# The last expert's second product in eight column tiles, with the FFN's first tiles loaded between them, and VectorE's order at two places

## The reference

```python
def expert_choice_moe(h, w_router, w_gate, w_up, w_down):
    ...
    a = jnp.einsum('becd,edf->becf', xg, w_gate)
    u = jnp.einsum('becd,edf->becf', xg, w_up)
    y = jnp.einsum('becf,efd->becd', jax.nn.silu(a) * u, w_down)
    y = y * top_w[..., None].astype(y.dtype)
    return ...scatter-add of y over the tokens...

x = x + g2 * expert_choice_moe(h2, ...)      # end of block one
return rms_norm(x, final_g)                  # into block two

f = swiglu(rmsnorm(h, g[0]), ffn_gate[i, 0], ffn_up[i, 0], ffn_down[i, 0])
h = h + MACARON * rmsnorm(f, g[1])
```

## Time and profile before

| | |
|---|---|
| time, median of 3 runs | 2323.99 us (2323.2 to 2325.95) |
| the profiled execution's own time | 2323.81 us |
| its span | 2322.5 us |
| TensorE busy | 2010.2 us (87%) |
| VectorE busy | 983.5 us (42%) |
| ScalarE busy | 669.7 us (29%) |
| DMA | 647.48 MB, mean 279 GB/s |
| chain that ended last, by engine | PE 51%, DMA 20%, SP's queue 17%, DVE 7% |

### The profile page before, as it was taken

One profiled execution on the slowest core, in us unless ns is written; L12 is line 12 of the kernel. 1 busy time (PEld: TensorE's weight loads), 2 busy tenths in 40 slices (PEclk: granted clock), 3 DMA queues, 4 the chain that ended last, 5 costly groups with the idle time before them and its releaser, 6 DMA issues.

```text
span 2322.5 us, 29242 instructions
## 1 busy us (share of the span) xinstructions
PE 2010.2 (87%) x12336; PEld 1339.5 (58%) x12336; DVE 983.5 (42%) x1219; ACT 669.7 (29%) x812; POOL 66.7 (3%) x144
## 2 busy tenths in 40 slices
PE   7999999666666666666678999999999999999998
PEld 4767972111111111111136999779998999788997
DVE  3744661000000000000004656876658656876656
ACT  3433430000000000000003444564435444465444
POOL 0000000000000000000001000000001000100000
PEclk8999999777777777777789999999999999999999
DMA  7345899999999999999998565335554554425552
GB/s 305 120 176 202 338 377 421 421 421 421 420 421 420 421 421 420 420 421 420 421 421 331 188 204 173 132 118 182 192 193 160 182 194 170 170 78 186 192 190 90
DMA packets 91363, 647.48 MB, mean 279 GB/s; under 512 B 10144, under 2 KB 10656, under 8 KB 14304
## 3 DMA queue, kind: packets, MB, share of 16 engines
q1 hardware_dynamic: 91232, 645.61, 71.2%
HBM read 644.52 MB, written 1.05 MB: 278 GB/s over the span
## 4 chain that ended last, share of the span: by engine, by line
PE 51%; DMA 20%; SPq 17%; DVE 7%; ACT 2%; issue 2%; POOL 1%; DVEq 0%; ACTq 0%; POOLq 0%
SPq L2821 16%; PE PS L449 13%; PE PS L451 13%; PE PS L450 13%; DMA XR<-in_mu 4%; DMA front<-in_mu 3%; PE PS L907 3%; DMA QT<-in_mu 2%; DMA XT<-in_mu 2%; DMA ring<-in_mu 2%; DMA ring<-in_fg 1%; DMA XT<-in_md 1%; DMA c_dft<-in_mu 1%; DVE low L1846 1%; DMA ring<-in_wq 1%
## 5 line engine op out<-in xcount | busy, mean ns | idle before, releaser
L1846 DVE TENSOR_TENSOR low<-ring,WH 128x2048 fp32r<-128x2048 f32 (+1 forms) x163 | 372.1, 2283 | 181.6 <-ACT WH L2235 179.1
L449 PE MATMUL PS<-XH,WH 128*128 128x256 f32 x1408 | 396.9, 282 | 3.6 <-DVE XL L1878 3.6
L450 PE MATMUL PS<-XL,WH 128*128 128x256 f32 x1408 | 395.1, 281 | 0.0
L451 PE MATMUL PS<-XH,low 128*128 128x256 f32 x1408 | 393.1, 279 | 0.0
L2235 ACT ACTIVATE WH<-ring 128x2048 fp32r<-128x2048 f32 (+1 forms) x164 | 313.1, 1909 | 29.2 <-DMA ring<-in_fg 22.9
L449 PEld LDWEIGHTS PS<-XH,WH 128*128 128x128 f32 x1408 | 264.5, 188 | 7.2 <-issue 5.4
L451 PEld LDWEIGHTS PS<-XH,low 128*128 128x128 f32 x1408 | 267.4, 190 | 0.0
L450 PEld LDWEIGHTS PS<-XL,WH 128*128 128x128 f32 x1408 | 264.6, 188 | 1.4
L1828 DVE TENSOR_TENSOR T1S<-T1S,PS 128x512 f32<-128x512 f32 x16 | 11.0, 688 | 536.6 <-PE PS L907 536.6
L2501 ACT ACTIVATE T1S<-PS 128x512 f32<-128x512 f32 x16 | 9.6, 597 | 547.7 <-PE PS L907 547.7
L449 PE MATMUL PS<-WH,FH 128*128 128x512 f32 x352 | 139.6, 396 | 0.4 <-DVE FL L1976 0.4
(11 more groups left out here) (453 smaller groups left out, 3132.9 us busy)
## 6 DMA issues: line engine op xcount, KB each, us to landing
ring<-in_fg SPq DMA_DIRECT2D x44, 1024.0 KB, 4.9
ring<-in_fu SPq DMA_DIRECT2D x44, 1024.0 KB, 4.9
ring<-in_fd SPq DMA_DIRECT2D x44, 1024.0 KB, 4.8
ring<-in_mu SPq DMA_DIRECT2D x39, 1024.0 KB, 26.9
ring<-in_md SPq DMA_DIRECT2D x39, 1024.0 KB, 27.1
ring<-in_mg SPq DMA_DIRECT2D x36, 1024.0 KB, 27.2
ring<-in_wmod SPq DMA_DIRECT2D x24, 1024.0 KB, 6.1
ahead<-in_mg SPq DMA_DIRECT2D x14, 1024.0 KB, 27.4
```

Source lines behind the costliest of these rows:

```text
L449: t.matmul(o, l[0], r[0], start=start, stop=False, skip_group_check=True)
L450: t.matmul(o, l[0], r[1], start=False, stop=False, skip_group_check=True)
L451: return t.matmul(o, l[1], r[0], start=False, stop=stop, skip_group_check=True)
L1846: own(v.tensor_tensor(low[:, w.slot.index, 0:size], w.flat, WH[:, w.slot.index, 0:size].bitcast(f32), ALU.subtract).then_inc(*c.wl.up()), ...
```

## The change

The second product of expert 15 is taken by output columns. Its 8 MB are laid out as eight tiles, each with all of the contraction for 128 output columns, and each column q goes through everything at once: product (16 matmuls into bank 2), T1, scatter into 128 columns of banks 4 to 7, copy to XR, two transposes into bank 3, then ScalarE scales by the final gain into XH and VectorE makes XL in one operation from the same bank. fg0 and fu0 are queued between md124, md125 and md126, their splits are made by ScalarE and VectorE behind columns 4 and 5, and the two first products of the FFN run as generators whose 16 steps (6 matmuls each) are handed out from column 5 on. `mu5` to `mu7` and the `md` tiles get other slots, and the first row load waits for `scat` 16, the first column's scatter, on SP ahead of fg1. The statistics behind it keep their order. At two places VectorE's order is changed.

```diff
-        todo = [(name, ex * 8 + k, count, 4 * ex + k // 2 + 1 + (ex == 15 and k > 5) if name == "md"
+        todo = [(name, ex * 8 + k, count, (61 + k if ex == 15 else 4 * ex + k // 2 + 1) if name == "md"
...
-        for n in range(13, 384):
+        for n in range(13, 368):
             load_expert(rest[(n - 13) % len(rest)], n)
...
+        for n, at in enumerate((4, 8, 7, 6, 9, 5, 10, 11)):
+            load_expert(wide[at], 368 + n)
+        for n in range(4):
+            load_expert(slots[2 + n], 376 + n)
+        load_expert(wide[12], 380)
...
+        load_split("fg", 0)
+        load_expert(wide[0], 381)
+        load_split("fu", 0)
+        load_expert(wide[1], 382)
+        load_expert(wide[3], 383)
+        row_slot[0].loads = wide[13].loads
...
-                if n < 11:
+                if n == 0 and f == 0:
+                    load_row(0, (c.scat, 16))
+                elif n < 11:
                     load_split("fg", f * 11 + n)
                     load_split("fu", f * 11 + n)
-                if n == 1 and f == 0:
-                    load_row(0, (c.scat, 17))
```

TensorE; `first_tile` waits for `rwv` k + 1 (XL of column k) ahead of its step k:

```diff
-            for j in range(2):
+            P.wait_ge(c.pw, 16)
+            for q in range(8):
+                w = W["md", 120 + q]
+                P.wait_ge(*w.landed)
+                P.wait_ge(c.yv, 30 + q)
+                tile = w.flat.rearrange("p (a b) -> p a b", a=16)
+                for i in range(4):
+                    for j in range(4):
+                        x = t.matmul(PS[32 * j:32 * j + 32, 2, 0:128], PT[:, 0, i * 128 + 32 * j:i * 128 + 32 * j + 32],
+                                     tile[:, 4 * i + j, :], start=i == 0, stop=i == 3, skip_group_check=True)
+                x.then_inc(*c.dn.up())
+                if q < 6:
+                    turn_over(1, 2)
+                if q == 6:
+                    step(gate, 1)
+                if q == 7:
+                    step(up, 1)
+                P.wait_ge(c.yv, 31 + q)
+                P.wait_ge(c.xsa, q)
                 for m in range(2):
...
+                x.then_inc(*c.scat.up())
+                if q < 6:
+                    turn_over(1, 2)
+                if q > 5:
+                    step(up, 1)
+                P.wait_ge(c.xsa, q + 1)
+                P.wait_ge(c.rwv, q)
+                for m in range(2):
+                    x = t.transpose(PS[:, 3, m * 128:m * 128 + 128], XR[:, m, q * 128:q * 128 + 128], ident[:, :])
+                x.then_inc(*c.rw.up())
+                if q == 5:
+                    step(gate, 5)
+            step(up, 1)
+            step(gate, 2)
+            step(up, 4)
```

VectorE, then ScalarE:

```diff
-            split_to(1)
-            for j in range(2):
-                for m in range(2):
-                    gains(m, j, 2 * m + j, fgc)
-                for m in range(2):
-                    low_rows(m, j, 2 * m + j)
-            split_to(2)
-            V.wait_ge(c.xsa, 4)
+            for q in range(8):
+                h = slice(q * 128, q * 128 + 128)
+                V.wait_ge(c.dn, 61 + q)
+                own(v.tensor_tensor(T1[:, h], PS[:, 2, 0:128], gB[:, 1, h], ALU.mult).then_inc(*c.yv.up()), c.yv)
+                V.wait_ge(c.rwa, V.nth(c.rwa))
+                own(v.scalar_tensor_tensor(XL[:, q, :], PS[:, 3, 0:256], fgc[:, q:q + 1], XH[:, q, :].bitcast(f32),
+                                           ALU.mult, ALU.subtract).then_inc(*c.rwv.up()), c.rwv)
+                if q in (4, 5):
+                    split_to(q - 3)
...
-            A.wait_ge(c.dn, 65)
-            split_to(1)
-            for j in range(2):
-                A.wait_ge(c.scat, 16 + j)
-                for m in range(2):
-                    own(copy(XR[:, m, j * 512:j * 512 + 512], PS[:, 4 + 2 * m + j, :]).then_inc(*c.xsa.up()), c.xsa)
...
+            for q in range(8):
+                h = slice(q * 128, q * 128 + 128)
+                A.wait_ge(c.scat, 16 + q)
+                own(copy(XR[:, :, h], PS[:, 4 + q // 4:8:2, q % 4 * 128:q % 4 * 128 + 128]).then_inc(*c.xsa.up()), c.xsa)
+                A.wait_ge(c.rw, A.nth(c.rw))
+                own(a.activation(XH[:, q, :], PS[:, 3, 0:256], ACT.Copy, scale=fgc[:, q:q + 1]).then_inc(*c.rwa.up()), c.rwa)
+                if q in (4, 5):
+                    split_to(q - 3)
             for m in range(2):
                 sum_square(XR[:, m, :], m)
             split_to(3)
```

The two places, in both layers:

```diff
                 masked(0)
+                split_to(tile("wid", 6 * l) + 6)
                 masked(1)
-                split_to(tile("wid", 6 * l) + 6)
...
+                rows(1, 0, gT[:, g0 + 16:g0 + 24])
                 w, s = factor(2, 0)
                 spread(0, w, s)
-                rows(1, 0, gT[:, g0 + 16:g0 + 24])
```

More of the change, by code:

```diff
@@ L935, in tensor_program @@
                 P.wait_ge(c.ht, ex + 1)
+                if ex == 15:
+                    break
                 for i in range(4):
@@ L1021, in ffn @@
                 for n in range(12):
-                    if n < 11:
+                    if n < 11 and (f or n):
                         for j, name in enumerate(("fg", "fu")):
@@ L1066, in added, with first_tile @@
                     held[4 + 2 * m] = held[5 + 2 * m] = [(c.xs, 4 * event + 2 * m + 1)]
-            for j in range(2):
-                for m in range(2):
-                    rows(m, j, 2 * m + j, XR, c.xsa, 2 * j + m + 1)
-            turn_over(4, 3)
+            def first_tile(name, b):
+                wh, wl = parts(name, 0)
+                for k in range(8):
+                    P.wait_ge(c.rwv, k + 1)
+                    for i in range(2):
+                        s = slice(i * 128, i * 128 + 128)
+                        x = mm3(PS[:, b, i * 256:i * 256 + 256], (wh[:, k, s], wl[:, k, s]), (XH[:, k, :], XL[:, k, :]),
+                                k == i == 0, k == 7)
+                    if k == 7:
+                        x.then_inc(*c.wu.up())
+                    yield 1
@@ new lines, in tensor_program, with step @@
+            gate, up = first_tile("fg", 0), first_tile("fu", 1)
+            def step(side, n):
+                for _ in range(n):
+                    next(side)
+            P.wait_ge(c.pw, 16)
[17 more added lines that the diff above has]
+                P.wait_ge(c.xsa, q)
+                for m in range(2):
+                    x = t.matmul(PS[:, 4 + 2 * m + q // 4, q % 4 * 128:q % 4 * 128 + 128], PB[:, 0, m * 128:m * 128 + 128],
+                                 T1[:, q * 128:q * 128 + 128], start=False, stop=True, skip_group_check=True)
+                x.then_inc(*c.scat.up())
[10 more added lines that the diff above has]
+                    step(gate, 5)
@@ L1072, in tensor_program @@
+            step(up, 1)
+            step(gate, 2)
+            step(up, 4)
+            held[0], held[1] = [(c.gr, 1)], [(c.hf, 1)]
+            held[2], held[3] = [(c.yv, 38)], [(c.rwv, 8)]
+            for b in range(4):
+                held[4 + b] = [(c.xsa, 8)]
+            for m in range(2):
+                for j in range(2):
+                    turned[m, j] = c.rw.n
             for l in range(2):
@@ L1832, in vector_program @@
                     V.wait_ge(c.scat, ex)
+                if ex == 15:
+                    break
                 for n in range(2):
                     h = slice(512 * n, 512 * n + 512)
-                    V.wait_ge(c.dn, 65 if ex == 15 and n else 4 * ex + 4)
+                    V.wait_ge(c.dn, 4 * ex + 4)
                     own(v.tensor_tensor(T1[:, h], PS[:, n, :], gB[:, 1, h], ALU.mult).then_inc(*c.yv.up()), c.yv)
@@ L2944, in layout @@
     d["md"] = np.ascontiguousarray(md.transpose(0, 3, 1, 4, 2, 5)).reshape(128, 128, 2, 1024)
+    columns = md[15].reshape(2, 2, 4, 128, 8, 128).transpose(4, 3, 2, 0, 1, 5)
+    d["md"][120:128] = columns.reshape(8, 128, 2, 1024)
     ng = I["norm_gains_2"]
```

25 lines of the change are left out of this document (6 added, 19 removed).

## The result

The changed kernel takes 2328.66 us (median of 13 runs, 2325.72 to 2329.71) against 2323.71 us for the kernel before in the same comparison (13 runs, 2321.77 to 2326.18): ratio 1.0019, 95% interval 1.0012 to 1.0027. It is 4.95 us slower by the medians, where +1.4 was forecast. The profiled execution took 2328.82 us, 5.01 more than the one of before.

| place | before | after | lag |
|---|---|---|---|
| VectorE's copy of PT (arrival at the seam) | 1228.41 | 1228.98 | 0.57 |
| first down product | 1279.50 | 1286.97 | 7.47 |
| layer 0's attention, past the masks (values) | 1501.65 | 1509.07 | 7.42 |
| second FFN of layer 0, its first product | 1569.08 | 1575.90 | 6.82 |
| end (own time) | 2323.81 | 2328.82 | 5.01 |

A forecast was written before the change was run, and what follows sets the result against it. The weights' stream bounds up to 1245 us, TensorE from 1258.5, neither in the seam between. Seam +1.7, clock +1.4 and VectorE's orders -1.7 make +1.4, so 2325.4 us on the median 2323.99; range 2319.5 to 2330.

The forecast's parts named there:

- The seam: Between the two blocks, until the first down product: +1.7 us, and +3.1 with the slow clock spell of 1.4.
- VectorE's orders: Two changed places of VectorE's order, masks and rows, in both layers: together -1.7 us.
- Loads: New slots and queue order cost nothing; md125 lands at 1242.9, the last md tile at 1250.4, fg0 at 1240.4.
- A column of 3.0 us: Each column's chain through three engines takes about 3.0 us, more than a tile's 2.49, so column 5 starts at 1244.2.
- the rival of rounds without overlap: Column products' rounds take 0.22 us instead of 0.11, adding +6.2 us, 2331.6; chance 0.12.
- The stand before column 5: TensorE stands 3.7 us, 1245.7 to 1249.45, because T1 of column 5 is queued behind VectorE's split of fg0.
- The clock: Behind the stand of 3.7 us, one half-rate spell in the gate's five steps: +1.4 us.
- second slow spell: A further stretch of slow clock, grouped with double waits as something else slower; joint chance 0.06.
- Columns 6 and 7 and the split of fg1: Column 7's XL at 1262.1, fg1's split ends 1268.3, TensorE waits 2.4 us, first down product 1.7 us late.
- the masks: wid split ahead of masked(1): TensorE's 0.97 us wait ends but mostly returns; gain 0.1 us a layer.
- the rows: rows(1, 0) ahead of factor and spread: XL comes 0.75 us earlier; gain 0.75 us a layer.
- the clock stays up: Rival: no slow spell behind the stand at the seam, 2324.0 us; chance 0.24.

The follow-up runs named there:

- e7: e4 with the next column's product put between scatter and transposes for the first four columns, fewer fillers, VectorE's next T1 ahead of XL; 2322.57 us, ratio 0.9993.
- e6: e4 without the filler matmuls behind the first six products and their scatters; 2326.89 us, ratio 1.0007 to the kernel before.
- e4: The changed kernel with VectorE splitting fg0 behind T1 of column 5 instead of ahead of it; 2324.33 us, ratio 1.0000 to the kernel before.
- e2: The changed kernel with VectorE's old order at masks and rows, so the seam's change alone; 2329.83 us, ratio 1.0027 to the kernel before.
- e3: The changed kernel with 14 more filler matmuls behind column 5's product and 8 ahead of the wait for fg1's split; 2326.18 us, ratio 1.0009.
- e5: e4 with ScalarE copying fg1 ahead of the two squares of XR instead of behind them; 2323.40 us, ratio 0.9995 to the kernel before.
- e9: e7 with the last two columns earlier among the FFN steps and fu0 split behind T1 of column 6; 2320.42 us, ratio 0.9984.
- e8: e7 with e5's edit, fg1 copied ahead of the squares; 2322.20 us, ratio 0.9988 to the kernel before.
- e1: The kernel before with only VectorE's two new orders, at masks and rows, in both layers; 2323.37 us, ratio 0.9995.
- e10: The changed kernel once more, unaltered, to see its clock in another execution; 2327.81 us, ratio 1.0018 to the kernel before.

## Why the prediction was right or wrong

The time was in the range and the ratio, 1.0019, just inside 0.2%, but the size was missed: +4.95 us for +1.4. That it came out inside is partly luck. The seam lost 6.9 us where 3.1 were forecast, and behind it 2.5 came back where 1.7 were, of which VectorE's orders gave only 1.2. Step by step:

**Loads: right.** fg0, fu0 and the `md` tiles are never what TensorE waits for in the changed kernel. In e7, which goes as fast as the tiles, column 5 starts at 1243.30 when its tile has landed (forecast 1242.9).

**A column of 3.0 us: wrong by 0.22, five times over.** The product's rounds are 0.11 us as taken (8 rounds in 1.08 us with the last one's end, 0.27), so the rival of rounds without overlap fell; the estimate of 0.107 for four loads in turn, from the Trainium skill (TensorE: Matmul & The Clock Gate, LDWEIGHTS), agrees with the round, but not part by part: here each load record of 32 columns lasts 0.11 us, and the four of a round lie side by side. From product to scatter it is 1.61 us (1239.40 to 1241.01) where 1.50 was worked out, from scatter to transposes 1.25 for 1.13, from transposes to the next product 0.36 for 0.31 and a little: the handovers were set too low, each by 0.05 to 0.1. (XH with its gain takes 0.47 us, not the 0.38 of a copy, but TensorE's column step does not wait for it.) Column 5 starts 16.12 us behind column 0, not 15.0: **+1.1 us**. e6 and e7 confirm that this is latency.

**The stand before column 5: right** in cause, place and length (3.63 for 3.7; split ended 1250.82 for 1249.05, later by the arrival and the columns). e4 shows it to be VectorE's order alone.

**The clock: right in cause, wrong in size.** One spell at 1.4 us was added, from the one row of an earlier stand. The half-rate stretch behind the first stand cost 2.5 us, for it lasted 6 us (1251.2 to 1257.35) of full work and not the 16 matmuls of that row; in e2, with the same work behind the same stand, it was shorter and cost 1.15. The second spell, 1.2 us, behind the wait for fg1, wasn't in the sum: the stand was forecast (2.4 us, measured 2.33), but it was not asked what the clock does behind it. The "second slow spell" had a share of 0.06 with others. Together 3.7 for 1.4: **+2.3 us**, the largest error, by the comparison with e3's clock of 1.00.

**Columns 6 and 7 and the split of fg1: right.** Columns 3.33 us apart (forecast 3.3), last XL 4.56 behind column 7's start (4.4), the split's end 6.13 behind the last XL (6.2). That the statistics and splits behind the last XR set the end of the seam is what e5, e7 and e9 bear out: e9 gains by an earlier last XL alone: counted from VectorE's copy of PT, it ends 2.25 us earlier than in e7, and the first down product comes 2.26 earlier. From the split to the first down product 12.9 us were forecast, and e4 has 12.80 (1267.72 to 1280.52). The path was VectorE's split of fu1 and then RB, as forecast, in the six runs of the changed seam that ran this piece at full clock (e3, e4, e5, e7, e8, e9). In e4:

```profile
1272.21 2.29 DVE L1914 TENSOR_TENSOR low<-ring,WH 128x2048 fp32r<-128x2048 f32 x1
1274.54 0.42 DVE L2035 COPY RB<-PS 128x256 f32<-128x256 f32 x1
```

In the changed kernel the bound is TensorE's 48 matmuls of fg1 at half rate: RB waits for the ones matmul (L1050) behind them.

```profile
1280.98 0.42 DVE L2033 COPY RB<-PS 128x256 f32<-128x256 f32 x1 [1.25 <-PE PS L1050]
```

That is how the second spell costs 1.2 us: up to the ones matmul it takes 1.5 (7.30 us for 5.76 in e4), and 0.3 of that is hidden behind VectorE.

**The arrival** of the profiled execution at the seam was 0.57 us later. The errors add up: 1.1 + 2.3 + 0.6, and 0.4 of small ones, make the first down product 4.4 us later than forecast (1286.97 for 1282.6).

**VectorE's orders: nearly right.** -1.7 forecast, -1.2 in e1's trace; the masks nothing instead of 0.1 a layer, the rows 0.6 to 0.7 instead of 0.75. The time of e1 alone, 0.9995 with 1.0 in its interval, can't tell this from no change. The other 1.3 us that came back behind the seam were in no term of the sum; most of them are the tile of layer 1 above.

**The rival "the clock stays up"** was given 0.24, and in the three profiles with the stand of 3.63 us nothing speaks for it; "slower by rounds" had the right sign for a wrong reason. Since two stands were forecast, two spells belonged in the sum, the second at least as a chance, and with both at 1.4 us the forecast would have been 2326.8.

## What to carry to other kernels

Cutting a product into pieces that each pass through several engines was worth it here only when the next piece's work filled the handovers (e7, 2.2 for 3.2 us a piece) and when no long operation was queued ahead of a short one that the next engine stood for (e4, 4.3 us for an operation of 0.29). For each stand of the bounding engine that a forecast contains, add what its clock may do behind it, as a chance and a price, and take the price by the full-rate work that follows, not from an earlier spell behind which less work lay. Before a gain or a loss is put down to an edit, look whether a spell came or stayed away in that one profile. And where the path behind the seam hangs on the last piece, bring the last piece forward, and put the work that nobody waits for behind it (e9).

## What the runs showed of the hardware

A stand doesn't by its length tell whether the clock falls. Behind a stand of 1.54 us at the same place e4 ran at a granted clock of 1.00 and e5 at 0.52, and behind the wait of 2.33 us for fg1 e4 and e7 ran at 1.00, the changed kernel and e10 at 0.94 over 27 us and e6 at 0.95. Windows of e5, then of e4:

```profile
1251.00:1254.50 3.50, 1.67 (x13) 1.25 (x12) 2.78 (x2) 2.85 (x4) 0.00 (x0) 1.00 1.02 421
1254.50:1258.00 3.50, 3.50 (x19) 3.50 (x18) 2.29 (x1) 0.43 (x1) 0.00 (x0) 0.52 0.83 346
```
```profile
1247.50:1251.00 3.50, 1.67 (x13) 1.27 (x12) 2.78 (x2) 2.77 (x3) 0.00 (x0) 1.00 1.00 414
1251.00:1254.50 3.50, 3.50 (x56) 3.33 (x54) 2.29 (x1) 0.00 (x0) 0.00 (x0) 1.00 0.98 407
```

Gaps of 0.5 us, on the other hand, twice in each 3.2 us, left it at 1.00 (e6).

Open is a tile of the second FFN in layer 0. ScalarE waits 1.05 us for its landing in the kernel before and 1.29 in the changed kernel, but 3.15 in e7, 3.25 in e8 and 2.61 in e9. In these three SP's issue just ahead of the tile's own took 1.73, 1.75 and 1.34 us, in the others 0.43. It is the same issue, of `in_wple`, that took 1.65 us in e3 in layer 1. It costs e7 to e9 one to two microseconds at the transposes behind (TensorE waits 1.71, 1.81 and 1.18 us there), which they would win on top. Why SP is slower there is not shown; the code around it is the same. In e6 the wait is 2.30 us with an issue of 0.43, so the issue isn't the whole of it.
